# An attention pipeline rebuilt: values product in high and low parts, all turned blocks split by ACT and DVE

## The reference

```python
# layer 0: 8 MLA heads and 8 FoX heads, both causal over the whole sequence
logits = einsum('bqhd,bkhd->bhqk', q, k) * scale       # FoX: + F[t] - F[s]
p = softmax(where(s <= t, logits, -1e30))
o = einsum('bhqk,bkhd->bqhd', p, v)                    # head size of v: 64
# layer 1, first group: 3 dilated groups (d1, d4, d16) x 4 heads, keys t, t-d, ..., t-w, position bias;
# each group's outputs are merged by softmax of the groups' log-sum-exp
out = einsum('gbhq,gbqhd->bqhd', softmax(lses), outs)
# layer 1, second group (nsa): 4 query heads, each over 63 compressed keys (cmp), all causal keys (sel)
# and a window of 512 (win), summed with three sigmoid gates
out = gb[..., 0:1] * o_cmp + gb[..., 1:2] * o_sel + gb[..., 2:3] * o_win
```

## Time and profile before

| | |
|---|---|
| median of 3 runs | 3389.16 us (3382.21 to 3389.79) |
| span of the profiled execution | 3393.3 us |
| PE busy | 3124.6 us, 92% of the span |
| DVE busy | 1348.8 us, 40% |
| POOL busy | 809.7 us, 24% |
| ACT busy | 727.8 us, 21% |
| mean granted clock of PE | 0.937 of full |

### The profile page before, as it was taken

One profiled execution on the slowest core, in us unless ns is written; L12 is line 12 of the kernel. 1 busy time (PEld: TensorE's weight loads), 2 busy tenths in 40 slices (PEclk: granted clock), 3 DMA queues, 4 the chain that ended last, 5 costly groups with the idle time before them and its releaser, 6 DMA issues.

```text
span 3393.3 us, 46007 instructions
## 1 busy us (share of the span) xinstructions
PE 3124.6 (92%) x14660; PEld 2555.4 (75%) x14660; DVE 1348.8 (40%) x2457; ACT 727.8 (21%) x1197; POOL 809.7 (24%) x466
## 2 busy tenths in 40 slices
PE   8897988898999999999999986688889999999999
PEld 5776888875888888876788875577758888888867
DVE  4634554505222222226433148876443222222254
ACT  2203433313100111113210022233331111111131
POOL 2330021321332332322233202100113233233222
PEclk9998987898999999999999986777799999999999
DMA  4236411100111111110135263344101111111101
GB/s 158 107 118 186 104 47 37 49 31 25 50 45 49 49 44 49 49 56 31 38 117 210 79 163 92 88 102 102 44 25 44 50 49 43 49 49 43 62 32 75
DMA packets 69611, 241.10 MB, mean 71 GB/s; under 512 B 9091, under 2 KB 12675, under 8 KB 68663
## 3 DMA queue, kind: packets, MB, share of 16 engines
q1 hardware_dynamic: 57992, 196.35, 19.4%
q10 hardware_dynamic: 11488, 43.16, 3.3%
HBM read 195.60 MB, written 48.59 MB: 72 GB/s over the span
## 4 chain that ended last, share of the span: by engine, by line
PE 79%; DVE 11%; issue 4%; ACT 3%; DMA 2%; SPq 0%; DVEq 0%; ACTq 0%; POOL 0%; POOLq 0%
PE ACC L895 59%; PE OP L1070 7%; PE ACC L1030 5%; PE TR L1045 4%; PE OP L951 3%; DVE R L1487 2%; DVE T L1510 1%; DVE H L1513 1%; DVE XL L1493 1%; PE TR L1082 1%; DVE T L1535 1%; ACT PT L1293 1%; DVE HL L1538 1%; DMA BIASD<-b_d 1%; ACT T L1267 1%
## 5 line engine op out<-in xcount | busy, mean ns | idle before, releaser
L792 POOL CAST WH<-RAW 128x1024 fp32r<-128x1024 f32 x203 | 215.8, 1063 | 1946.1 <-PE ACC L895 1755.7
L895 PE MATMUL ACC<-XH,WH 128*128 128x512 f32 x1792 | 581.6, 406 | 52.4 <-DVE XL L1493 38.4
L895 PE MATMUL ACC<-XL,WH 128*128 128x512 f32 x1792 | 556.8, 392 | 0.0
L895 PE MATMUL ACC<-XH,WL 128*128 128x512 f32 x1792 | 555.7, 391 | 0.0
L794 POOL TENSOR_TENSOR WL<-RAW,WH 128x1024 fp32r<-128x1024 f32 x203 | 495.4, 2440 | 24.2
L895 PEld LDWEIGHTS ACC<-XH,WH 128*128 128x128 f32 x1792 | 337.9, 190 | 158.8 <-issue 75.9
L895 PEld LDWEIGHTS ACC<-XL,WH 128*128 128x128 f32 x1792 | 338.9, 189 | 71.7
L895 PEld LDWEIGHTS ACC<-XH,WL 128*128 128x128 f32 x1792 | 338.7, 189 | 71.8
L1542 DVE TENSOR_TENSOR M<-M,ACC 128x1024 f32<-128x1024 f32 x128 | 156.3, 1221 | 520.8 <-PE ACC L895 520.8
L895 PE MATMUL ACC<-HH,WH 128*128 128x512 f32 x1024 | 322.2, 396 | 17.0 <-DVE HL L1538 17.0
L1265 ACT ACTIVATE HH<-T 128x1024 fp32r<-128x1024 f32 x64 | 68.0, 1062 | 1168.5 <-DVE T L1535 1168.5
(11 more groups left out here) (188 smaller groups left out, 3339.9 us busy)
## 6 DMA issues: line engine op xcount, KB each, us to landing
RAW<-in_w SPq DMA_DIRECT2D x203, 512.0 KB, 3.2
QK<-y_odds SPq DMA_DIRECT2D x128, 256.0 KB, 5.1
y_odds<-HALVES ACTq DMA_DIRECT2D x16, 1024.0 KB, 5.0
QK<-y_foxs SPq DMA_DIRECT2D x48, 256.0 KB, 5.6
y_foxs<-HALVES ACTq DMA_DIRECT2D x8, 1024.0 KB, 4.7
y_kv<-Q ACTq DMA_DIRECT2D x8, 512.0 KB, 2.6
BIAS<-y_f SPq DMA_DIRECT2D x4, 1024.0 KB, 8.3
y_odd<-HALVES ACTq DMA_DIRECT2D x8, 512.0 KB, 2.6
```

Of the source, the lines that this page charges most:

```text
L792: nc.gpsimd.tensor_copy(WH[:, slot], RAW[:, slot]).then_inc(s_whi, 1)
L895: mm = nc.tensor.matmul(acc[:, h * HALF:(h + 1) * HALF], w(k), x[:, k, h * HALF:(h + 1) * HALF], start=first and k == k0 and w is ws and x ...
```

## The change

The attention part is written anew; projections, MLP and gate stay.

- Order: one unrolled sequence of steps for each layer, in place of the loops. Even: 4 fox jobs, then 4 MLA jobs of two heads. Odd: d1, d4, d16, cmp for pair 0, the same for pair 1, then sel, win, sel, win. The merge is cut into 14 pieces, one for each following step, so it lies beside the compressed job. All waits are for constants.
- Values: V is split into high and low parts (VS, 128 columns for a head: high and low side by side) and is the stationary operand. The turned probabilities are split too (PT high by ACT out of TR, PT low by DVE as TR minus high) and move, two query blocks (a chunk) at once, 256 columns. The output lies turned already (64 x tokens), its main part in one half of the partitions and the correction in the other.
- Sums: for each half head (four tasks) one reciprocal, and four matmuls against IDENT that spread the values over the partitions (`norm`); for dilated jobs POOL spreads sum and minimum first. ACT copies the correction, DVE adds it and multiplies; POOL splits the result into XH and XL.
- The plan has a second kind of group, "B" (ACT copies the block to SBUF, POOL splits it); the planner here sets every group to kind "A".
- Memory: the attention uses H's place for probabilities, bias and V, so ACT loads H again behind each attention: the input in layer 0, and in layer 1 a copy that it stores to memory in the gate's tiles of layer 0. Four score buffers and eight probability buffers for small tasks, two and three for large ones.

The core of the diff:

```diff
-        "fox": (2, [("fox", 2, 0, 0), ("fox", 2, 1, 1)]),
-        "mla": (4, [("mla", 2, 0, 0), ("mla", 2, 1, 1)]),
+EVEN_JOBS = [("fox", p) for p in range(4)] + [("mla", p) for p in range(4)]
+ODD_JOBS = ([(k, 0) for k in DILATED] + [("cmp", 0)] + [(k, 1) for k in DILATED] + [("cmp", 1)]
+            + [("sel", 0), ("win", 0), ("sel", 1), ("win", 1)])
...
+                for g0 in range(0, len(st.turn.blocks), 4):
+                    kind = "A"
+                    st.turn.groups.append(group(g0, min(4, len(st.turn.blocks) - g0), kind))
...
     PE
-                            mm = nc.tensor.matmul(OP[:, b, 0:HD], lhs, rhs, start=x == 0,
-                                                  stop=x == len(t["blocks"]) - 1)
+                def values(c):
+                    j, col = c.job, c.c % 2 * 256
+                    pe.wait_ge(s_ptD, c.d)
...
+                    if c.opens:
+                        wait(pe, s_o, c.half.no)
+                    order = sorted(c.keys, key=lambda x: x[1] - x[2])
+                    for n, (k, c0, c1) in enumerate(order):
+                        for hl in range(2):
+                            v, pt = VS[:, j.slot, k, c.e * P:(c.e + 1) * P], PT[:, c.buf, hl, k - c.k0, c0:c1]
...
+                            mm = nc.tensor.matmul(OP[:, 0, col + c0:col + c1], v, pt,
...
+                def norm(h):
+                    pe.wait_ge(s_rl, h.rl)
...
+                    for m, t in enumerate(h.tasks):
...
+                            rows = RL[:, t.col:t.col + 1].to_broadcast([P, P])
+                        mm = nc.tensor.matmul(OP[:, 1, m * P:(m + 1) * P], rows, IDENT[:], start=True, stop=True)
     ACT
+                def correction(h):
+                    act.wait_ge(s_pv, h.chunks[1].no + 1)
...
+                    nc.scalar.activation(CORR[rows], OP[other, 0], ACT.Copy).then_inc(s_cor, 1)
...
+                        wait(act, s_pv, c.no - 1)
+                        nc.scalar.activation(PT[0:r, c.buf, 0, k0:k0 + g.n, m * P:(m + 1) * P],
+                                             src.rearrange("p (k q) -> p k q", q=P), ACT.Copy).then_inc(s_ptA, 1)
...
+                for c in range(DC):
+                    act.dma_start(H[:, c], src[c]).then_inc(s_hre, 16)
     DVE
+                        dve.wait_ge(s_ptA, g.a)
+                        V_.tensor_tensor(lo, TR[0:r, g.ring, 0:g.n * P].rearrange("p (k q) -> p k q", q=P),
+                                         hi.bitcast(F32), ALU.subtract).then_inc(s_ptD, 1)
...
+                    V_.reciprocal(r, L[:, c0:c0 + 4]).then_inc(s_rl, 1)
...
+                    V_.tensor_tensor(dst, OP[rows, 0], CORR[rows], ALU.add).then_inc(s_o1, 1)
+                    dve.wait_ge(s_o1, h.o1)
+                    dve.wait_ge(s_nrm, h.no + 1)
+                    V_.tensor_tensor(dst, dst, OP[rows, 1], ALU.mult).then_inc(s_o, 1)
     POOL
+                    nc.gpsimd.tensor_copy(xh, total).then_inc(s_xo, 1)
+                    pool.wait_ge(s_xo, h.xo)
+                    nc.gpsimd.tensor_tensor(xl, total, xh.bitcast(F32), ALU.subtract).then_inc(s_xl, 1)
```

More of the change, by code:

```diff
@@ L179, in at @@
     return idx0 if step == 0 or isinstance(it, int) and it == 0 else it * step + idx0
-TASK0 = 2 * NB
 DILATED = ("d1", "d4", "d16")
 NSA = ("cmp", "sel", "win")
[L188 to L220, removed]
-    def blocks(self, i):
-        k = self.kind
-        if k in ("fox", "mla", "sel"):
-            return list(range(i + 1))
-        if k == "win":
-            return list(range(max(0, i - WIN_BLOCKS), i + 1))
-        if k == "d1":
-            return list(range(max(0, i - 1), i + 1))
-        if k == "d4":
-            return [i - 1, i] if i % 2 else [i]
-        return [i] if k == "d16" else [0]
-    def width(self, i):
-        return HD if self.kind == "cmp" else P * len(self.blocks(i))
@@ L542, in program @@
         tcount = {"m0": 0, "n0": 8, "m1": 16, "n1": 24}
-        TASKS_EVEN = phases["mla"][1][-1][-1].c1
-        TASKS_ODD = phases["nsa"][1][-1][-1].c1
-        COPIES = {name: rows[-1][-1].ogroups[-1]["rel"][1] for name, (_, rows) in phases.items()}
+        EVEN, ODD = phases["even"].end, phases["odd"].end
         segs_first = {n: segs[g].iters[0][0] for n, g in
@@ L840, in _ @@
+                for st in ph.steps:
+                    if st.split:
+                        split_head(*st.split)
+                    if st.turn:
+                        split_turned(st.turn)
+                        if st.turn.i % 4 == 3 and st.turn.kind in DILATED:
+                            spread_sums(st.turn.half)
+                    if st.out:
+                        outputs(st.out)
+                    for p, k in st.merge:
+                        merge(p, k)
             for name in ("in0a", "in0p", "in0b", "in0c", "up0"):
@@ L867, in _ @@
                 weights(name)
-            run(pool, 2, merge)
+            attention("odd")
             weights("out1")
@@ L1148, in _ @@
             pe.wait_ge(s_rt, 3)
[L1149 to L1154 removed]
+            attention("even")
             layer_end(0)
@@ L1384, in _ @@
             tile_loop("up0", store)
-            attention("fox")
-            attention("mla")
+            last = tiles[seg_end["up0"] - 1]
+            for k in range(2):
+                act.wait_ge(s_store[k], 16 * last.store[k])
+            act.wait_ge(s_misc, 32)
+            act.wait_ge(s_rope, ROPE_KEY_STEPS + 2 * NB)
+            attention("even")
+            reload_h("even", ins["xT"])
             def layer_end(l):
@@ new lines, in attention @@
+                for st in ph.steps:
+                    if st.start:
+                        low_v(st.start)
+                    if st.logits:
+                        scores(st.logits)
+                    if st.out:
+                        outputs(st.out)
+                    for p, k in st.merge:
+                        merge(p, k)
+                    if st.turn:
+                        low_turned(st.turn)
+                        if st.turn.i % 4 == 3:
+                            inverse_sums(st.turn.half)
```

1038 lines of the change are left out of this document (556 added, 482 removed).

## The result

The changed kernel takes 3430.9 us (median of 4 runs, 3426.9 to 3435.0) against 3385.7 for the kernel before, timed beside it: a ratio of 1.0138, 95% interval 1.0121 to 1.0155. It is slower by 1.4%, where 3251 was forecast. The profiled execution has a span of 3425.1 us.

What follows compares the result with a forecast made beforehand. Inside an attention pipeline PE was taken to bound the kernel, nearly all its time work. 3393.3 less 84 (even stretch) and 54 (odd) gave 3255, and 4 less for profiling 3251 us; range 3180 to 3350.

Steps and rivals of the forecast that it cites:

- Unit costs: Single instructions in attention: subtraction of 512 columns 688 ns, values matmul of 256 columns 0.11 us, sums 0.11 per instruction.
- the sum: Work per fox head in the changed kernel, added up by engine: PE 14.6 us, DVE 14.5, ACT 13.9.
- Head time: Attention heads, from the busiest engine of each of eight steps: 18.4 fox and 19.5 MLA, taken as 18 and 19 us.
- V's turning: Turning V for a job: 0.4 us a head on PE, 0.6 each on ACT and DVE.
- The check of the rule: Busiest engine per step, applied to a fox head of the kernel before: 18.0 us against 16.8 measured, so queues smooth some.
- rival (b): Handovers rule: 0.4 us more on each even, selected and window step, dilated heads at 12.5: 3340 us; chance 0.15.
- Drains: Even stretch: pipeline run-downs between iterations go, only heads replace them; stretch 330 us against 414, 84 less.
- Dilated jobs: Odd stretch, dilated heads: no clear gain on 11.4 to 11.9 us a head, 138 for both pairs (140 before).
- Compressed jobs and merges: Odd stretch: merges spread over the compressed steps, 28 merge, 14 heads, 7 latencies: 49 us each, 98 for both.
- The start: Time to a stretch's first score: 19 us in the even stretch, 24 in the odd one.
- the tail's 15: End of the even stretch, last exponential to output split and first output weights on POOL: 15 us.
- rival (c): PE, waiting more, gets its full clock less often; even stretch equals today's at 0.65; at 0.6, 3414 us; chance 0.10.

Runs made afterwards that it cites:

- experiment 8: Changed kernel with next scores ahead of values and sums on PE, and in dilated jobs the first output step not waiting for ACT's copy of sums: 3276.8 us (0.968).
- experiment 9: Kernel of experiment 8 with V turned in two pieces in a job's third and fourth step: 3298.4 us; with V turned for each layer's first two jobs alone: 3241.6.

## Why the prediction was wrong, step by step

**Unit costs: right.** The subtraction of 512 columns took 687 ns (688 said), sixteen values matmuls in a row 2.1 us where 0.11 each make 1.8, eight instructions of sums 1.11 (0.9 said). Groups of the changed kernel:

```profile
L1742 DVE TENSOR_TENSOR PT<-TR,PT 128x512 fp32r<-128x512 f32 x140 | 94.6, 687 | 48.9 <-ACT PT L1388 46.4
```

POOL was at work beside 40 of the 140, which took as long as the others. The rule of the Trainium skill ("GPSIMD Engine Reference", section Specifications) is on two SBUF inputs; these have one and an operand in PSUM, so it rightly stayed out of the sum. One reading there was loose: the additions of the earlier trace rows ran beside POOL's splits in 64 of 128 cases, half and not most. Busy times bear the sum out: in the window of two fox heads DVE has 30.3 us and ACT 27.2, 15.2 and 13.6 a head for the 14.5 and 13.9 of the sum. PE shows 37.1, with 0.93 of the clock: 18.5 a head for the 14.6 of the sum. Its busy spans overlap, so this is no price; at full clock it is 33.3 for two heads (experiment 8), 16.7 each, and the kernel before shows 19.1 for a head priced at 16.3.

**Head time: the step that failed.** "I added up, over the eight steps of a head, the busiest engine of each step" assumes that in a step all engines work at once and wait for none. In the changed program PE's order made values and sums of one chunk stand ahead of the next scores, and these feed DVE. That edge isn't between steps but inside one, and the sum left it out: fox and MLA heads took 23.7 and 24.2 us in place of 18 and 19, and the edge is 4.6 of a fox head (47.4 against 38.2 a pair) and 3.8 of an MLA head (48.5 against 40.9). With scores ahead and the early output step, and V left out, the heads measured 18.0 and 18.9, as the forecast; it had V in, though, and with V they are 19.1 and 20.2, above its own 18.4 and 19.5. So the rule holds for a program whose order gives it the slack, V's turning apart, and this one doesn't. I had the piece for it: "PE makes scores s, turns s-2, and every second step does the values" was written down, but only as amounts.

**The check of the rule: badly chosen.** "For the kernel before that gives 18.0 where 16.8 was measured, so queues smooth some of it." The head of the earlier trace rows is the first of its iteration, and the pipeline fills during it: up to the next head's first scores only 34 of its 72 values matmuls have run (two for each block), and the clock was at 0.70. A usual head has all of them in its interval. Windows of the kernel before with the values matmuls alone (L1070: us, PE, PEld, clock, DMA share, GB/s), that head and the next:

```profile
385.38:402.19 16.81, 5.40 (x34) 5.51 (x34) 0.70 0.22 64
402.19:422.25 20.06, 9.20 (x75) 8.66 (x73) 1.00 0.57 150
```

The three heads behind it, in the timeline of DVE:

```profile
422.25 0.29 DVE L1629 CUSTOM_DVE_ANT_0 PB<-ACC,BIAS 128x128 f32<-128x128 f32 x1 [2.32 <-PE TR L1045]
...
443.16 0.29 DVE L1629 CUSTOM_DVE_ANT_0 PB<-ACC,BIAS 128x128 f32<-128x128 f32 x1 [0.60 <-PE TR L1045]
...
476.93 0.29 DVE L1629 CUSTOM_DVE_ANT_0 PB<-ACC,BIAS 128x128 f32<-128x128 f32 x1 [5.36 <-PE ACC L1030]
```

From 402.19: 20.1, 20.9, and 33.8 with the drain. A usual head took 20 to 21, above the rule's 18; "a head stood at 1.03 of PE's work" set a half-filled interval against a whole head's work, and a usual head stood at 1.2 to 1.3 of it. Four intervals would have shown that handovers cost 2 to 3 us even there, and with that rival (b), 3340, would have had more than 0.15. It is also too low: its 0.4 us a step is 3.2 a head, and 5 to 6 came.

**V's turning: mis-sized.** Counted 0.4 on PE and 0.6 each on ACT and DVE, beside other work; it costs 2.5 us a job (experiment 9), as it goes through the ring in series. That part of the sum counted engine time and left out the waits between the three engines.

**Drains.** "Where the drains go, nothing comes in their place but the head itself": right as a mechanism, drains of 10 to 15 us each are gone. But every head of the pipeline now costs more, and the even stretch ends 6.4 us shorter (407.4 from its last projection matmul, 413.8 before).

**Dilated jobs.** "No clear gain on 11.4 to 11.9" added up each engine and not the end of a half head, which comes every four small tasks: sums of 2.0 at half clock, copy, two output steps of 1.1. With the queue on PE and the needless wait for DL it was 16 to 17 a head. With both taken out the first pair is at 11.8 a head (70.5, against 71.6 before), but the second at 12.7 (76.3, against 68.2): 147 for both where 138 were forecast and 140 taken before.

**Compressed jobs and merges: right in the number, in part by luck** (98.2 for 98). Of the 49 each, 42 were DVE's work and 7 latencies; DVE was busy for 39.5 of the first one's 48.5, so 9 were waits, part of them from the same queue on PE: in experiment 8 DVE is busy for as long and the two take 87.3. The start was right: 18.8 (19) and 21.0 (24). The even stretch's last head and tail took 38.3 for 34. PE's first output matmul waits for POOL's weights, 6.91 and 8.24 us in the rows above, but the tail's 15 had this in; with scores ahead head and tail take 33.6, so the 4 us are again the head's.

**The clock, rival (c): not the cause in the even stretch.** It sat at 0.92 there, above the 0.87 before and far from the 0.65 from which it was to decide. In the dilated pair it was a little lower than before, 0.69 against 0.74. It moves with the program: the fox window went from 0.93 to 1.00 and the dilated pair from 0.69 to 0.87 when PE stopped waiting (experiment 8). That is the direction of the rule cited from the Trainium skill ("TensorE: Matmul & The Clock Gate", Part 1), that idling lowers it; so part of each gain above is clock. How much wasn't separated, least of all in the dilated jobs.

Windows of the kernel of experiment 8, two fox heads and the first dilated pair:

```profile
389.00:427.20 38.20, 33.33 (x256) 30.92 (x256) 29.77 (x71) 26.75 (x63) 7.30 (x7) 1.00 0.56 135
1928.00:1998.50 70.50, 60.42 (x367) 56.52 (x367) 51.29 (x169) 54.94 (x167) 6.78 (x11) 0.87 0.60 138
```

So the changed kernel's lost 168 us are in the order of work on PE and one wait that is too wide, and in V's turning, each with what the clock gave back beside it: these edits alone bring the kernel from 3430.9 to 3265.0. Open: the cost of its last 14 us over the forecast (3265 against 3251), why later values and V in pieces help only together, and how much of the dilated jobs' time is clock.

## What to carry to other kernels

A sum of the busiest engine per step prices a program only if its order on each in-order engine lets the steps overlap: walk through one step's queue of each engine and ask for every instruction what stands in front of it and whether the next engine waits for what is behind. Put what feeds another engine ahead of what only finishes older work. When checking such a rule against a trace, take all heads of the loop, not one; and a wait that shows little time in the trace may be hidden behind another, so that it only gains once that one is gone.

## What was unexpected of the hardware

The sums' eight fp32 instructions of 128 columns take 1.11 us at full clock and 2.02 at half, and they stand at the end of a half head, where in the rows of experiment 8 ACT's copy and then DVE's output steps wait for them: at half clock this end weighs double. DVE's addition for DU, 64x512 from OP, takes 0.68 to 0.70 us in d1, where it writes side by side, and 1.06 to 1.08 in d4 and d16, where the same instruction writes to every fourth or eighth place; ACT's copy of the sums goes from 0.59 to 1.1 in the same way. The sum had DVE's outputs of these jobs at 4 us a head, and that is about right (two steps of 1.07 in each half head).
